# Twenty inverse square roots on GpSimd as one power, in a two-layer hybrid decoder step on one Trainium2 core

## What is computed

```python
def _rms(x, g):
    xf = x.astype(jnp.float32)
    y = xf * lax.rsqrt(jnp.mean(xf * xf, axis=-1, keepdims=True) + EPS)
    return (y * g.astype(jnp.float32)).astype(x.dtype)
...
k = _rms(k.reshape(b, m, MEM_HEADS, MEM_HD), k_g)              # memory keys, 64 wide
k = _rms(k.reshape(b, t, DIFF_HEADS, 2, DIFF_HD), k_g)         # shared keys, 64 wide
q = _rms(qf.reshape(b, t, DIFF_HEADS, 2, DIFF_HD), P['q_norm'][j])
mq = _rms(mq.reshape(b, t, MEM_HEADS, MEM_HD), P['mem_q_norm'][l])
```

## Time and profile before

| | |
|---|---|
| Median of 3 runs | 1599.25 us (1593.43 to 1603.15) |
| Profiled execution: span from first to last instruction | 1595.4 us; its own time is not given apart from the span |
| PE busy | 1467.6 us (92%) |
| DVE busy | 959.0 us (60%) |
| ACT busy | 577.3 us (36%) |
| POOL busy | 119.7 us (8%) |
| Chain that ended last, by engine | PE 72%, DVE 17%, ACT 5%, issue 3% |

### The profile page before, as it was taken

How to read it: one execution, slowest core, us unless ns; L and a number is a source line. 1 busy time by engine, 2 the same in 40 slices (tenths; PEclk the granted TensorE clock), 3 DMA queues, 4 the chain that set the end, 5 groups by cost and what they waited for, 6 DMA issues and landing times.

```text
span 1595.4 us, 27270 instructions
## 1 busy us (share of the span) xinstructions
PE 1467.6 (92%) x10820; PEld 1393.1 (87%) x10820; DVE 959.0 (60%) x1827; ACT 577.3 (36%) x949; POOL 119.7 (8%) x133
## 2 busy tenths in 40 slices
PE   4899867899999999999999996888999999999997
PEld 3799765789999999999888884765999999999997
DVE  4789888556663664466767775217366635653662
ACT  3444434444431222223445554125243322221232
POOL 2000103210000000001100003211010000000001
PEclk8899997789999999999999998998899999999999
DMA  7121222122233233222322224431123233233222
GB/s 208 42 65 54 93 79 81 30 66 82 85 87 93 85 87 93 81 85 74 91 73 60 68 65 167 165 104 53 40 80 93 80 92 93 80 93 88 85 74 67
DMA packets 208538, 134.87 MB, mean 85 GB/s; under 512 B 4971, under 2 KB 201152, under 8 KB 208391
## 3 DMA queue, kind: packets, MB, share of 16 engines
q1 hardware_dynamic: 201319, 105.30, 23.0%
q0 software_dynamic: 7120, 28.18, 5.4%
HBM read 126.24 MB, written 7.85 MB: 84 GB/s over the span
## 4 chain that ended last, share of the span: by engine, by line
PE 72%; DVE 17%; ACT 5%; issue 3%; DMA 1%; SPq 1%; POOL 0%; POOLq 0%; ACTq 0%; DVEq 0%
PE acc L485 55%; PE acc L662 6%; DVE conv_out L1478 3%; ACT w_hi L999 2%; PE acc L963 2%; DVE w_lo L1385 2%; PE psX L751 1%; PE psX L946 1%; DVE softmax_stats L1864 1%; ACT exps L1288 1%; DVE turned L1402 1%; DVE root_row L1411 1%; PE psT L696 1%; SPq L398 1%; PE psX L844 1%
## 5 line engine op out<-in xcount | busy, mean ns | idle before, releaser
L485 PE MATMUL acc<-xa_hi,w_hi 128*128 128x272 f32 x1824 | 384.8, 292 | 10.6 <-DVE xa_lo L1416 10.1
L485 PE MATMUL acc<-xa_hi,w_lo 128*128 128x272 f32 x1824 | 378.7, 289 | 0.0
L485 PE MATMUL acc<-xa_lo,w_hi 128*128 128x272 f32 x1824 | 377.6, 289 | 0.0
L999 ACT ACTIVATE w_hi<-w_raw 128x1024 fp32r<-128x1024 f32 x194 | 205.4, 1059 | 383.1 <-PE acc L485 306.5
L485 PEld LDWEIGHTS acc<-xa_hi,w_hi 128*128 128x128 f32 x1824 | 289.1, 189 | 13.1 <-issue 10.2
L1385 DVE TENSOR_TENSOR w_lo<-w_raw,w_hi 128x1024 fp32r<-128x1024 f32 x194 | 237.6, 1225 | 84.8 <-ACT w_hi L999 83.2
L485 PEld LDWEIGHTS acc<-xa_lo,w_hi 128*128 128x128 f32 x1824 | 288.3, 190 | 0.0
L485 PEld LDWEIGHTS acc<-xa_hi,w_lo 128*128 128x128 f32 x1824 | 286.2, 190 | 0.0
L485 PE MATMUL acc<-xb_hi,w_hi 128*128 128x272 f32 x832 | 174.8, 291 | 2.0 <-DVE xb_lo L1812 2.0
L485 PE MATMUL acc<-xb_hi,w_lo 128*128 128x272 f32 x832 | 172.1, 288 | 0.0
L485 PE MATMUL acc<-xb_lo,w_hi 128*128 128x272 f32 x832 | 171.6, 288 | 0.0
(11 more groups left out here) (298 smaller groups left out, 1989.3 us busy)
## 6 DMA issues: line engine op xcount, KB each, us to landing
w_raw<-in_w_up SPq DMA_DIRECT2D x88, 512.0 KB, 3.9
w_raw<-in_w_down SPq DMA_DIRECT2D x32, 512.0 KB, 3.9
w_raw<-in_w_in_a SPq DMA_DIRECT2D x14, 512.0 KB, 4.3
w_raw<-in_w_down SPq DMA_DIRECT2D x16, 384.0 KB, 3.3
w_raw<-in_w_kv SPq DMA_DIRECT2D x12, 512.0 KB, 3.8
k_pages<-in_cache_k POOLq DMA_DIRECT2D x16, 384.0 KB, 4.3
v_pages<-in_cache_v POOLq DMA_DIRECT2D x16, 384.0 KB, 3.9
w_raw<-in_w_mem_kv SPq DMA_DIRECT2D x8, 512.0 KB, 3.9
```

The costliest lines, as they stand in the source:

```text
L485: last = nc.tensor.matmul(acc[slot][:, c, 0:n], w, x[:, k, c * n:(c + 1) * n], start=(k == 0 and q == 0), stop=(k == kb - 1 and q == 2))
L999: nc.scalar.activation(whi[:, slot % 2, :], wraw[:, slot, :], ACT.Copy).then_inc(w_hi_ready, 1)
```

## The change

The twenty roots of the query and key tiles no longer use ACT's square root and DVE's reciprocal. DVE's `tile_root_row` makes the variance as before and raises a new semaphore; GpSimd takes the variance to the power -0.5 in one operation of 17 (or 8) numbers per partition, with the exponent from a small constant tile; DVE waits for that and spreads the result. The other seven roots keep the old way. GpSimd's program gets the twenty powers at the places where the tiles come, and whatever stands behind one of them waits for it.

```diff
+        mhalf, _ = place("minus_half", [P, 8])
...
+        tile_var, tile_root = sem("tile_var"), sem("tile_root")
...
             def tile_end(s):
                 kind, t, nq = tiles[s]
                 if kind != "v":
-                    root(cols_of(s))
                     return
...
+            def tile_root_row(src, nq, n, read, beside):
+                w = n // 32
+                nc.vector.transpose(t1[:, 0:n], src).then_inc(read[0], 1)
+                dve.wait_ge(*read)
+                nc.vector.tensor_scalar(small[:, 0, 0:w], t1[:, 0:n].rearrange("p (a b) -> p a b", b=32)[:, :, 0],
+                                        1.0 / MHD, EPS, ALU.mult, ALU.add).then_inc(tile_var, 1)
+                if beside:
+                    beside()
+                dve.wait_ge(tile_root, nq + 1)
+                link(nc.vector.transpose(rr[:, 0:n], small[:, 2, 0:w].unsqueeze(2).broadcast_to((P, w, 32))))
+                settle()
...
-                root(psum2(acc[s % 2], n), n, 1.0 / MHD, EPS, rr[:, 0:n], read=(acc_free, s + 1),
-                     beside=(lambda: conv(3)) if s < S_OUT[0] else None)
+                tile_root_row(psum2(acc[s % 2], n), nq, n, (acc_free, s + 1),
+                              (lambda: conv(3)) if s < S_OUT[0] else None)
...
+            def roots(cols, count):
+                w = cols // 32
+                for _ in range(count):
+                    nroot[0] += 1
+                    pool.wait_ge(tile_var, nroot[0])
+                    nc.gpsimd.tensor_tensor(small[:, 2, 0:w], small[:, 0, 0:w], mhalf[:, 0:1].broadcast_to((P, w)), ALU.pow
+                                            ).then_inc(tile_root, 1)
...
             add_squares("n0")
+            roots(T, MC)
+            roots(MEM, MC)
             pool.wait_ge(mm_done, S_MEM)
...
             memory_values_out(0)
+            roots(MEM, MC)
             memory_keys_out(0)
...
             for h in range(H):
+                roots(T, 1)
                 pool.wait_ge(acc_free, S_B + 3 * h + 2)
...
+                roots(T, 1)
...
+            roots(T, MC)
             pool.wait_ge(mm_done, S_B + 20)
```

More of the change, by code:

```diff
@@ L1995, in _ @@
             pool.memset(ones[:, :], 1.0).then_inc(zeroed, 1)
+            pool.memset(mhalf[:, :], -0.5)
             pool.memset(uext[:, :, 0:TAPS - 1], 0.0).then_inc(zeroed, 1)
@@ L2011, in add_squares @@
                     ins.then_inc(sq_used, 1)
+            nroot = [0]
+            def roots(cols, count):
[5 more added lines that the diff above has]
+                                            ).then_inc(tile_root, 1)
             def cache_rows(which, l, b_):
```

## The result

The changed kernel takes **1641.06 us** (median of 4 runs, 1639.20 to 1641.89) against 1599.17 us of the kernel before in the same session (4 runs, 1593.43 to 1603.15): a ratio of **1.0271, 95% interval 1.0247 to 1.0295**. It is slower, as forecast, but by 41.9 us instead of 12, and 5 us above the upper end of the range. The profiled execution has a span of 1640.2 us, 44.8 more than before.

The account below looks back on a forecast made before the run. Bound: PE overall, the DVE-ACT chain of waits in the attention stage, DVE in the memory stage. Terms 10.5 - 0.3 + 1.8 + 0 = +12.0 us on 1595.4 + 3.85 gave 1611 us; range 1594 to 1636.

Parts of the forecast that it names:

- D itself: Duration of one GpSimd power of 17 numbers per partition, taken as 1.32 us from an add over 544 numbers.
- second rival: Power on GpSimd works number by number without overlap: at 3 us each, +36 us, 1636 us; chance 0.22.
- the sum: Whole kernel's change for any D: 14.6 D - 7.3 us, +12.0 us at D = 1.32.
- dear power: The second rival: a power on GpSimd of 3 us, kernel time 1636 us; chance 0.22.
- Each exposed root costs D - 0.37: Attention stage: each of 11 roots on the chain takes D - 0.37 us more, +10.5 us in all.
- The last root, D + 0.20 instead of 1.85: Last root of the attention stage: variance to transpose 1.52 us instead of 1.85, -0.3 us.
- Memory stage, 0.66 of GpSimd's time lost by DVE: Memory stage: DVE loses 3.5 us beside 5.3 us of powers, saves 1.7 of reciprocals: +1.8 us.
- The clearings and page loads, 0 give or take 2: GpSimd's queue: clearings come 13 us later, page loads start near 975 us, hidden; 0, give or take 2 us.
- The third rival: Memory stage: PE's 8.7 us of waits for tap diagonals come off, 1602.5 us with D = 1.32; chance 0.08.
- Range and chances: Whole kernel: 1594 us (D = 0.15) to 1636 (D = 3); slower by over 0.5% 0.54, within 0.39, faster 0.07.

Follow-up runs that it names:

- price run: Kernel before, with eight operations (powers of several sizes, a multiply, an add) on idle GpSimd at the start; 1595.58 us.
- the cheap multiply: Changed kernel with a multiplication by -0.5 in place of each of the twenty powers, same places and waits; 1589.94 us, ratio 0.9952.
- the experiment: Changed kernel with powers in the memory stage only (6 tiles), square root and reciprocal kept elsewhere; 1601.02 us, ratio 1.0018.
- e8_cover: Changed kernel with DVE doing the next score blocks' mask, maximum and negative between variance and wait in the attention stage; 1606.45 us, ratio 1.0053.

## Why the prediction was wrong

**The step that failed is *D itself*: 1.32 us taken, 3.06 measured.** I counted 20 to 30 steps per number, each at the 0.003 us that an add takes for a number, so 0.06 to 0.09 us. The price run shows 0.16 us per number, and 0.54 us even for a single one. The estimate from dependent steps that stood beside the second rival, 3.4 us from the Trainium skill's "GPSIMD Engine Reference", section 7, was the nearer one, and the one of 0.45 us from its section 3.1 was far off; but the assumed sixty steps were mine, and no run shows the steps. With D = 3.06 the sum reads 14.6 x 3.06 - 7.3 = +37.4 us; measured +41.9.

**A term was left out of the sum: PE's clock.** I named it only beside the rival of the dear power, without a price. By the added matmuls it is some 10 to 12 us: PE idle for 3.06 us behind a query tile, then at little over half speed through work that stands on the chain. With it the sum would be 47 to 50 us, at the top of what was measured (39.5 to 47.2) or above it, so that the sum without it came as near as 4.5 us in part by luck: its term for the memory stage was 3.5 us too large, below. Point by point:

- *Each exposed root costs D - 0.37*: right in form. Measured 3.18 - 0.57 = 2.61, where it gives 2.69. The overlap was not quite right: of the two roots that hid behind PE's steps, the second no longer does, and moves the root behind it by another 1.8 us (its variance came 4.23 us later than before, that of the next root 6.05).
- *The last root, D + 0.20 instead of 1.85*: right. Variance to transpose went from 1.85 to 3.17 us, +1.3, where the formula gives +1.4. What the other removed table loads were worth (the traces have 54 loads before and 31 after), no run separates: with the cheap multiply the kernel gained 8.3 us where the sum gives 4.2 at D = 0.21, and they may be part of that.
- *Memory stage, 0.66 of GpSimd's time lost by DVE*: wrong in who waits for whom. At D = 3.06 the sum has 6.3 us for it (12.1 us of powers by 0.66, less 1.7); the experiment shows +2.75. The timelines of the changed kernel, GpSimd first, then DVE:

```profile
180.73 3.53 POOL L2036 TENSOR_TENSOR small<-small,minus_half 128x17 f32<-128x17 f32 x1 [143.48 <-DVE small L1420]
...
207.51 2.07 POOL L2036 TENSOR_TENSOR small<-small,minus_half 128x8 f32<-128x8 f32 x1 [9.06 <-DVE small L1420]
...
1018.17 2.01 POOL L2109 MEMSET mem_q_padded<- 128x2304 f32 x1
```

```profile
180.57 2.07 DVE L1492 SCALAR_TENSOR_TENSOR conv_out<-glu_ext,params,conv_out 128x512 f32<-128x512 f32 x3
184.29 0.75 DVE L1425 STREAM_TRANSPOSE root_row<-small 128x544 f32<-128x544 f32 x1 [1.66 <-POOL small L2036]
...
209.62 0.45 DVE L1425 STREAM_TRANSPOSE root_row<-small 128x256 f32<-128x256 f32 x1 [0.20 <-POOL small L2036]
...
1018.60 1.73 DVE L1887 TENSOR_SCALAR probs<-exps,softmax_stats 128x256 f32<-128x256 f32 x1
```

  Three taps beside a power take 2.07 us, some 0.7 each, as the taps without one; it is the power that stretches, from 3.06 to 3.53 and from 1.63 (alone) to 2.07. What is lost is plain waiting, 1.66 us at a power of 17 numbers and 0.20 at one of 8: the taps cover about half of the long power and all but 0.20 us of the short one. That is one of the signs that the prediction named for being wrong, a DVE that waits in the memory stage although its taps ran through.
- *The clearings and page loads, 0 give or take 2*: right. The second clearing now meets the weights instead of the softmax statistics (the last rows of both timelines above): the operation beside it takes 1.73 us. It takes 0.35 us elsewhere, so the clearing costs 1.4 us here, where it cost 1.85 before. PE waits 0.91 us ahead of the first page, for DVE's copy and not for a load, as before.
- *The third rival*: its evidence was read rightly. PE's waits for the tap diagonals, 8.7 us in three places, shrank to one of 0.5, and the memory stage was not shorter: from 172 to 254 us DVE is busy for 67.1 of 82 us and waits for 9.8 on the weights and 4.1 on the powers, so it still is the limit.
- *Range and chances*: the upper end was set at D = 3 without the clock. With the same D and a clock term of 10 us it would have held the time. The dear power at 0.22 deserved more, since no row spoke against a price per number far above an add's.

What stays open: some 5 us of the gain of `e8_cover`, why the changed kernel's heads are by turns about 35 and 37 us long, and what GpSimd does in the 0.16 us of a number. The additive account (45.4 us for the two stages apart, 44.8 between the profiled spans, 41.9 by the medians) closes within its intervals and no closer.

## What to carry to other kernels

Before an operation is moved to an engine on which it has never run in the trace, time it there by itself on an idle stretch; a count of its arithmetic steps at the rate of an add was off by more than a factor of two here, and at an exposed wait every microsecond counts. Where an engine hands something away and waits for it, first look for its own next independent work to put in between: here that took back 32 to 35 us of the loss, and made the kernel before 9.4 us faster. And where a wait on the chain also idles PE, add the slower matmuls behind it to its price: here 10 to 12 us on 32.

## What the runs showed of the hardware that I had not expected

- A power on GpSimd costs 0.54 us for one number per partition and 0.16 us for each further one, the same on 16 as on 128 partitions; a multiply of the same 128x17 takes 0.20 us.
- Adding sixty matmuls whose results nothing reads made the changed kernel 10 to 12 us faster, as the granted clock of the stage went from 0.90 to 1.00.
- DVE's taps, which lost 3.22 us to GpSimd's adds, lost nothing to its powers; the power lost 0.47 us. The Trainium skill, page "SBUF — State Buffer", section "Who interferes with whom", says that issue order decides who blocks, and that the one behind blocks for the whole instruction. At the adds the trace agrees: the one tap of the four that began before the first add, at 244.97, took 0.75 us, and the three that began while an add ran took 1.81 to 1.82. At the power only the first half shows: the tap that began before it, at 180.57, was not slowed, and the power took 0.47 us longer; but the tap that began at 181.89, inside the power (180.73 to 184.26), took 0.74 us as well. So GpSimd's power did not hold up DVE for its whole length; why is not shown.
